# The up blocks' tiles turned by VectorE's 32x32 stream transposes and a trip through DRAM instead of TensorE's turns

## Chip, cores and metric

One core of a Trainium2 chip. The metric is the device time of one execution in microseconds; the median of several executions is given. Lower is better.

## What is computed

Two transformer-like blocks on 256 tokens of width 2048, all in float32, one after the other. What matters here are their two feed-forward parts (`ffn(1, ...)` and `ffn(2, ...)` in the kernel, d_ff = 5632):

```python
h2 = _rmsnorm(x, ffn_norm_w[l])                                     # f = 1
g, u = jnp.split(jnp.einsum('bsd,df->bsf', h2, w_gate_up[l]), 2, axis=-1)
x = x + jnp.einsum('bsf,fd->bsd', jax.nn.silu(g) * u, w_down[l])
...
h2 = _rms(x, g_norm2) * (1 + sc2) + sh2                             # f = 2
gate, up = jnp.split(h2 @ w_ffn_in, 2, axis=-1)
x = x + gt2 * ((jax.nn.silu(gate) * up) @ w_ffn_out)
```

The second block also needs `c_act @ w_ada`, a product with one row (2048 x 12288) that depends on none of the rest.

## The kernel before

**Products.** Each weight matrix is streamed once in units of 1 MB (`raw`, 512 rows by 512 columns, four buffers). A unit has two chunks of 256 rows. For each chunk ScalarE rounds to a high half `whi` (line 903) and VectorE subtracts to get the low half `wlo` (line 1304); four chunk buffers. TensorE forms high x high, high x low and low x high (lines 866 to 868) for two token halves `m` and two k-tiles: 12 products of 128x128 by 128x512 for a chunk. One chunk is one *visit*, and visits set the order of everything: each engine's program is a loop over *slots*, and slot s does its part of visit s. The halves of a chunk are made three visits ahead: in slot s ScalarE casts, and VectorE subtracts, the chunk of visit s+2, whose buffer comes free with the end of visit s-2. On VectorE a slot is: low half, steps of `ada_tiles`, then side work. On ScalarE it is cast, then side work. On TensorE side work comes ahead of the products.

**w_ada.** VectorE forms the one-row product itself, from units of `w_ada` that go through the same four raw buffers (line 1761, two steps in each of two slots per unit). A `w_ada` unit stands after every second weight unit through the whole first feed-forward and the first four of the second one's gate/up pairs (to the middle of the fourth); later there are none.

**Feed-forward.** The 5632 hidden columns are eleven blocks of 512, in parts of six and five. For each j a gate block (8 visits) and an up block (8 visits), then for the part four down blocks of 12 or 10 visits, each over all the hidden columns of the part, in order. Side work of a block is counted by t, from the slot after its last visit: ScalarE's sigmoid and VectorE's multiply for a gate block at t = 0; for an up block, VectorE's multiply at t = 0 (lines 1474, 1476) into `ffn_tmp` (128 tokens by 512 columns, token half m), TensorE's eight turns at t = 2 (line 567 through `turn`, into a PSUM side bank), ScalarE's high half `aH` at t = 2 (line 978), VectorE's low half `aL` at t = 3 (line 1483). `aH` and `aL` (hidden columns on the partitions, tokens along the free axis) are the stationary operands of the down blocks.

**Loads.** SP issues one load per unit in order (line 2094). Load u waits until VectorE has finished with unit u-4 in the same buffer. `after(s)` is the first unit u whose buffer comes free in slot s or later. For an up block whose last visit is e, with `w_ada` units between: unit u-5's buffer comes free in slot e+2, unit u-4 is the `w_ada` unit of slot e+3, u-3 comes free in e+4, and u itself is cast in slots e+7 and e+8. Without them u-4 comes free in slot e+4 and u is cast in slots e+11 and e+12. Here u = `after(e + 3)`.

## Time and profile before

| | |
|---|---|
| median of 3 runs | 2470.77 us (2470.37 to 2470.88) |
| the profiled execution | 2470.06 us, span 2468.2 us |
| TensorE busy | 2460.1 us (100%), granted clock full |
| VectorE, ScalarE, GpSimd busy | 1754.4 (71%), 1191.7 (48%), 26.0 us (1%) |
| chain that ended last | 99% TensorE |
| DMA | 580 MB, 235 GB/s mean, 66% of the engines' time |

The span runs from the first to the last instruction in the trace. Engine rows add up the time in which an instruction of the engine was active. The chain is followed back from the last instruction, at each step to what released it. DVE is VectorE, ACT ScalarE, PE TensorE, PEld its weight loads, SPq the queue from which SP issues DMAs.

### The profile page before, as it was taken

What the parts mean: (1) busy time and instruction counts of PE and PEld (TensorE: products, weight loads), DVE (VectorE), ACT (ScalarE), POOL (GpSimd) and SP (SyncE); (2) the same over time, 40 slices, a digit from 0 to 9 for tenths busy, and PEclk for the clock granted to TensorE, in tenths of its full rate; (3) what the DMA queues carried; (4) which work ended last, traced back from release to release, by engine and by line L of the source; (5) the groups of instructions that cost most, each with busy time, mean ns of one, the idle gap of its engine ahead of it and who ended that gap; (6) DMA issues with size and microseconds to landing.
All of it is one profiled execution on the core that took longest, in us unless ns stands there. A gap on an engine that the chain in (4) does not pass through costs nothing.

```text
span 2468.2 us, 29482 instructions
## 1 busy us (share of the span) xinstructions
PE 2460.1 (100%) x11860; PEld 2158.6 (87%) x11860; DVE 1754.4 (71%) x2173; ACT 1191.7 (48%) x1459; POOL 26.0 (1%) x27
## 2 busy tenths in 40 slices
PE   9999999999999999999999999999999999999999
PEld 8898888888888888888888888888888888888888
DVE  7887798788888788886666465467788765555555
ACT  6545544544444444445765554444644444444443
POOL 0000000000000000000010000000000000000000
PEclk9999999999999999999999999999999999999999
DMA  8656666788888888886455445555588756555564
GB/s 304 236 194 233 224 215 245 257 317 299 289 304 304 307 292 300 303 295 249 164 189 182 155 171 188 205 190 189 190 295 296 286 187 205 201 197 202 193 202 151
DMA packets 82775, 580.27 MB, mean 235 GB/s; under 512 B 9424, under 2 KB 9808, under 8 KB 13264
## 3 DMA queue, kind: packets, MB, share of 16 engines
q1 hardware_dynamic: 82496, 578.28, 66.3%
q8 instruction: 94, 1.54, 0.2%
q14 instruction: 41, 0.34, 0.0%
q10 hardware_dynamic: 144, 0.12, 0.0%
HBM read 576.26 MB, written 2.10 MB: 234 GB/s over the span
## 4 chain that ended last, share of the span: by engine, by line
PE 99%; DVE 0%; DMA 0%; ACT 0%; issue 0%; SPq 0%; POOL 0%; ACTq 0%
PE bank L866 31%; PE bank L867 31%; PE bank L868 31%; PE bank L567 2%; PE bank L647 1%; PE bank L685 0%; DMA raw<-in_w_in_dram 0%; PE bank L696 0%; PE bank L697 0%; PE bank L666 0%; PE bank L655 0%; PE bank L665 0%; PE bank L686 0%; PE bank L708 0%; PE bank L757 0%
## 5 line engine op out<-in xcount | busy, mean ns | idle before, releaser
L1304 DVE TENSOR_TENSOR wlo<-raw,whi 128x1024 fp32r<-128x1024 f32 x885 | 1079.3, 1222 | 622.2 <-ACT whi L903 618.0
L903 ACT CAST whi<-raw 128x1024 fp32r<-128x1024 f32 x885 | 927.2, 1049 | 924.4 <-PE bank L868 907.1
L866 PE MATMUL bank<-whi,hH 128*128 128x512 f32 x2528 | 970.1, 384 | 1.9 <-DVE wlo L1304 1.4
L868 PE MATMUL bank<-whi,hL 128*128 128x512 f32 x2528 | 958.1, 379 | 0.0
L867 PE MATMUL bank<-wlo,hH 128*128 128x512 f32 x2528 | 958.1, 379 | 0.0
L866 PEld LDWEIGHTS bank<-whi,hH 128*128 128x128 f32 x2528 | 477.9, 189 | 69.2 <-DVE wlo L1304 1.8
L868 PEld LDWEIGHTS bank<-whi,hL 128*128 128x128 f32 x2528 | 477.8, 189 | 67.8
L867 PEld LDWEIGHTS bank<-wlo,hH 128*128 128x128 f32 x2528 | 478.1, 189 | 65.1
L1761 DVE SCALAR_TENSOR_TENSOR adacc<-raw,stat,adacc 128x512 f32<-128x512 f32 x360 | 269.5, 749 | 6.8
L866 PE MATMUL bank<-whi,aH 128*128 128x512 f32 x704 | 267.4, 380 | 0.0
L867 PE MATMUL bank<-wlo,aH 128*128 128x512 f32 x704 | 266.8, 379 | 0.0
L868 PE MATMUL bank<-whi,aL 128*128 128x512 f32 x704 | 266.8, 379 | 0.0
L868 PEld LDWEIGHTS bank<-whi,aL 128*128 128x128 f32 x704 | 133.1, 189 | 18.9
L867 PEld LDWEIGHTS bank<-wlo,aH 128*128 128x128 f32 x704 | 133.1, 189 | 18.7
L866 PEld LDWEIGHTS bank<-whi,aH 128*128 128x128 f32 x704 | 133.1, 189 | 18.7
L567 PE MATMUL bank<-ident,tmp 128*128 128x128 f32 x514 | 71.4, 273 | 0.2
L567 PEld LDWEIGHTS bank<-ident,tmp 128*128 128x128 f32 x514 | 61.4, 141 | 10.8 <-issue 0.9
L866 PE MATMUL bank<-whi,mH 128*128 128x512 f32 x128 | 49.2, 384 | 0.0
L867 PE MATMUL bank<-wlo,mH 128*128 128x512 f32 x128 | 48.5, 379 | 0.0
L868 PE MATMUL bank<-whi,mL 128*128 128x512 f32 x128 | 48.5, 379 | 0.0
L978 ACT CAST aH<-bank 128x512 fp32r<-128x512 f32 x44 | 23.8, 592 | 41.5 <-PE bank L567 41.5
L2016 POOL TENSOR_TENSOR stat<-stat 128x4 f32<-128x4 f32 (+2 forms) x22 | 24.0, 1098 | 1729.9 <-DVE stat L1324 1006.7
(311 smaller groups left out, 1416.7 us busy)
## 6 DMA issues: line engine op xcount, KB each, us to landing
raw<-in_w_gu_dram SPq DMA_DIRECT2D x176, 1024.0 KB, 4.9
raw<-in_w_ada_dram SPq DMA_DIRECT2D x96, 1024.0 KB, 4.9
raw<-in_w_down_dram SPq DMA_DIRECT2D x88, 1024.0 KB, 4.8
raw<-in_w_in_dram SPq DMA_DIRECT2D x60, 1024.0 KB, 4.8
raw<-in_w_in2b_dram SPq DMA_DIRECT2D x56, 1024.0 KB, 4.8
raw<-in_w_out_dram SPq DMA_DIRECT2D x32, 1024.0 KB, 4.8
raw<-in_w_in2a_dram SPq DMA_DIRECT2D x8, 1024.0 KB, 4.9
raw<-in_w_mla_dram SPq DMA_DIRECT2D x8, 1024.0 KB, 4.8
```

Of the source, the lines that this page charges most:

```text
L567: return e.transpose(o, i, ident[0:n, 0:n])
L647: ins = e.matmul(o[:, P * hd:P * hd + P], KC[:, base:base + P], qq, start=True, stop=True)
L866: e.matmul(o, xh[:, kt, sl], pairs(wh, i), start=k == 0, stop=False)
L867: e.matmul(o, xh[:, kt, sl], pairs(wl, i), start=False, stop=False)
L868: ins = e.matmul(o, xl[:, kt, sl], pairs(wh, i), start=False, stop=k == n - 1)
L903: e.copy(whi[i][:, :, :], raw[u % RAW][:, 2 * hf:2 * hf + 2, :]).then_inc(*ev("act_hi", c, 0))
L978: e.copy(aH[:, k0:k0 + 4, P * m:P * m + P], v4(side(b.index, m))).then_inc(*ev("act_half", b.index, m))
L1304: e.tensor_tensor(wlo[i][:, :, :], raw[u % RAW][:, 2 * hf:2 * hf + 2, :], f(whi[i][:, :, :]), ALU.subtract).then_inc(*ev("dve_lo", c, 0))
L1761: ins = e.scalar_tensor_tensor(d, src, col, d, ALU.mult, ALU.add)
L2016: e.tensor_tensor(sc(o, n), sc(i, n), sc(b_half, n), ALU.pow).then_inc(*ev("pool_pow", *key))
```

## The change

In an up block VectorE multiplies at t = 0 into a new tile `FT`, in an order in which each group of 32 columns is made of pieces that belong together, then turns every 32x32 block at t = 1 with two stream transposes into `ffn_tmp`. SP stores the two tiles to a DRAM scratch (`across`, 2 x 256 KB), waits for both stores, and loads them back with four transfers, one per 32 partitions, that put the 32x32 blocks where the full transpose has them, into `FT`. The pieces moved are 512 bytes. SP does this ahead of load `after(pl.last + 3)`. ScalarE makes `aH` from `FT` at t = 6 and VectorE `aL` at t = 7. The down blocks wait for `aL` itself. For f = 1 one factor `r2` moves from the up block's multiply into the gate block's, as its square.

```diff
--- before.py
+++ after.py
@@ -373,6 +373,8 @@
         gtB = new("gtB", [P, D])
         gR = new("gR", [P, 2, 16], F32R)
         AUX = [new("aux", [P, 512]), T[4]] + AD
+        FT = new("turned", [P, 2, 512])
+        across = nc.dram_tensor("across", (2, 2, P, 512), F32, kind="Internal").ap()
 
 
         top[0] = arena
@@ -464,6 +466,7 @@
         sem_first = [sem(f"s_first{i}") for i in range(5)]
         sem_xT = [sem(f"s_xT{i}") for i in range(7)]
         sem_x1, sem_vec, sem_late, sem_pos = sem("s_x1"), sem("s_vec"), sem("s_late"), sem("s_pos")
+        sem_away, sem_back = sem("s_away"), sem("s_back")
         sem_ident, sem_fw, sem_am, sem_out = sem("s_ident"), sem("s_fw"), sem("s_am"), sem("s_out")
 
 
@@ -492,6 +495,7 @@
         b_nr = {"q": cols(16), "k": cols(16)}
         b_ni = {k: cols(8) for k in (("q", 0), ("q", 1), ("k", 0), ("k", 1))}
         b_mx = [cols(6) for _ in range(3)]
+        b_rr = cols(2)
 
         def f(ap):
             return ap.bitcast(F32)
@@ -501,6 +505,14 @@
 
         def v8(t):
             return t[:, :].rearrange("p (a b) -> p a b", a=8)
+
+        def by_token(ap):
+
+            return ap.rearrange("p k (i t) -> p i k t", t=32)
+
+        def in_turn(m):
+
+            return FT[:, m, :].rearrange("p (i k t) -> p i k t", i=4, k=4)
 
         def tok_half(t3, m):
             return t3.rearrange("p (a b) -> p a b", a=4)[:, :, P * m:P * m + P]
@@ -548,6 +560,12 @@
 
             return 5 if b.index == 0 else 0
 
+        ups = [b for b in blocks if b.kind == "fup"]
+
+        def landed(b):
+
+            return sem_back, 64 * (ups.index(b) + 1)
+
         def hlev(u):
 
             lev = (u - 3) // 3 - 1
@@ -596,14 +614,6 @@
                 elif kind == "out" and t in (2, 3):
                     e.wait_ge(*on("dve_x1", b.index, 1))
                     turn_pair(lambda m: x[:, m, :], 4 * b.arg[0] + 2 * (t - 2), (b.index, t - 2))
-                elif kind == "fup" and t == 2:
-                    f_, j = b.arg
-                    for m in range(2):
-                        e.wait_ge(*acc_read(b, m))
-                        o = next_bank(e, b.index, m)
-                        for k in range(4):
-                            ins = turn(o[:, P * k:P * k + P], ffn_tmp(j, m)[:, P * k:P * k + P])
-                        ins.then_inc(*ev("pe_turn", b.index, m))
                 elif kind == "latent" and t == 4:
                     for p2 in range(2):
                         e.wait_ge(*on("act_lat", b.index, 1))
@@ -809,8 +819,8 @@
                     e.wait_ge(*side_read(pl.at["out", kt // 4].index, kt % 4 // 2))
                 elif b.kind == "fdown" and b.arg[2] == 0 and i == 0 and kt % 4 == 0 and m == 0:
                     up = pl.at["fup", b.arg[0], PARTS[b.arg[1]][0] + kt // 4].index
-                    e.wait_ge(*side_read(up, 0))
-                    e.wait_ge(*side_read(up, 1))
+                    e.wait_ge(*on("dve_aL", up, 0))
+                    e.wait_ge(*on("dve_aL", up, 1))
                 elif (b.kind == "latent" and b.arg == (0,) or b.kind == "fgate" and b.arg == (2, 0)) and (
                         i == 0 or (kt, m) == (1, 1)):
                     w = 0 if b.kind == "latent" else 1
@@ -970,12 +980,12 @@
                     for m in range(2):
                         e.activation(plain(ffn_tmp(j, m)[:, :]), summed(b, m), ACT.Sigmoid, bias=0.0,
                                      scale=sc(b_r2 + m) if f_ == 1 else 1.0).then_inc(*ev("act_sig", b.index, m))
-                elif kind == "fup" and t == 2:
+                elif kind == "fup" and t == 6:
                     f_, j = b.arg
                     k0 = 4 * (j - PARTS[j >= 6][0])
-                    for m in range(2):
-                        e.wait_ge(*on("pe_turn", b.index, m))
-                        e.copy(aH[:, k0:k0 + 4, P * m:P * m + P], v4(side(b.index, m))).then_inc(
+                    e.wait_ge(*landed(b))
+                    for m in range(2):
+                        e.copy(by_token(aH[:, k0:k0 + 4, P * m:P * m + P]), in_turn(m)).then_inc(
                             *ev("act_half", b.index, m))
                 elif kind == "fdown" and b.arg[:2] == (1, 1) and b.arg[2] < 3 and t == 1:
                     j = b.arg[2]
@@ -1457,31 +1467,42 @@
                     scaled_low(hH, hL, (b.index, t - 3), 4 * b.arg[0] + 2 * (t - 3), "ffn_norm_w")
                 elif kind == "fgate" and t == 0:
                     f_, j = b.arg
+                    if b.arg == (1, 0):
+                        e.wait_ge(*on("pool_pow", "r2"))
+                        e.tensor_tensor(sc(b_rr, 2), sc(b_r2, 2), sc(b_r2, 2), ALU.mult).then_inc(*ev("dve_small", "rr"))
+                        e.wait_ge(*on("dve_small", "rr"))
                     for m in range(2):
                         d, o = plain(ffn_tmp(j, m)[:, :]), summed(b, m)
                         e.wait_ge(*on("act_sig", b.index, m))
                         if f_ == 1:
-                            e.scalar_tensor_tensor(d, o, sc(b_r2 + m), d, ALU.mult, ALU.mult).then_inc(*acc_free(b, m))
+                            e.scalar_tensor_tensor(d, o, sc(b_rr + m), d, ALU.mult, ALU.mult).then_inc(*acc_free(b, m))
                         else:
                             e.tensor_tensor(d, o, d, ALU.mult).then_inc(*acc_free(b, m))
                 elif kind == "fup" and t == 0:
                     f_, j = b.arg
+                    n = ups.index(b)
                     e.wait_ge(*visit(end))
                     for m in range(2):
-                        d, o = plain(ffn_tmp(j, m)[:, :]), summed(b, m)
                         e.wait_ge(*acc_read(pl.at["fgate", f_, j], m))
-                        if f_ == 1:
-                            e.scalar_tensor_tensor(d, o, sc(b_r2 + m), d, ALU.mult, ALU.mult).then_inc(*acc_free(b, m))
-                        else:
-                            e.tensor_tensor(d, o, d, ALU.mult).then_inc(*acc_free(b, m))
-                elif kind == "fup" and t == 3:
+                        if n:
+                            e.wait_ge(*on("dve_aL", ups[n - 1].index, m))
+                        for i in range(2):
+                            s = ffn_tmp(j, m)[:, S * i:S * i + S].rearrange("p (k q c) -> p k q c", k=2, q=4)
+                            d = FT[:, m, :].rearrange("p (q k c) -> p k q c", q=4, k=4)[:, 2 * i:2 * i + 2, :, :]
+                            o = acc(b, m)[:, :].rearrange("p (k q c i) -> p i k q c", k=2, q=4, i=2)[:, i, :, :, :]
+                            ins = e.tensor_tensor(d, o, s, ALU.mult)
+                        ins.then_inc(*acc_free(b, m))
+                elif kind == "fup" and t == 1:
+                    for m in range(2):
+                        e.wait_ge(*acc_read(b, m))
+                        e.transpose(ffn_tmp(b.arg[1], m)[:, :], FT[:, m, :]).then_inc(*ev("dve_turned", b.index, m))
+                elif kind == "fup" and t == 7:
                     f_, j = b.arg
                     k0 = 4 * (j - PARTS[j >= 6][0])
                     for m in range(2):
-                        sl = slice(P * m, P * m + P)
+                        hi, lo = (by_token(w[:, k0:k0 + 4, P * m:P * m + P]) for w in (aH, aL))
                         e.wait_ge(*on("act_half", b.index, m))
-                        e.tensor_tensor(aL[:, k0:k0 + 4, sl], v4(side(b.index, m)), f(aH[:, k0:k0 + 4, sl]),
-                                        ALU.subtract).then_inc(*side_free(b.index, m))
+                        e.tensor_tensor(lo, in_turn(m), f(hi), ALU.subtract).then_inc(*ev("dve_aL", b.index, m))
                 elif kind == "fdown" and b.arg[:2] == (1, 0) and t == 0:
                     j = b.arg[2]
                     e.wait_ge(*visit(end))
@@ -2062,6 +2083,21 @@
                     e.wait_ge(*visit(SK[0] + 16))
                     e.dma_start(amask[:, :, :].rearrange("p a b -> p (a b)"), a["amask"]).then_inc(sem_am, 16)
 
+            def turn_across(u):
+
+                for n, b in enumerate(ups):
+                    if u == after(pl.last[b.index, 1] + 3):
+                        if n >= 2:
+                            e.wait_ge(*landed(ups[n - 2]))
+                        for m in range(2):
+                            e.wait_ge(*on("dve_turned", b.index, m))
+                            e.dma_start(across[n % 2, m], ffn_tmp(b.arg[1], m)[:, :]).then_inc(sem_away, 16)
+                        e.wait_ge(sem_away, 32 * (n + 1))
+                        rows = across[n % 2].rearrange("m (i p) (q c) -> q p m i c", i=4, q=4)
+                        for q in range(4):
+                            e.dma_start(FT[32 * q:32 * q + 32, :, :].rearrange("p m (i c) -> p m i c", i=4),
+                                        rows[q]).then_inc(sem_back, 16)
+
             def after(s):
 
                 return next(u for u in range(RAW, len(pl.units)) if pl.unit_free(u - RAW) >= s)
@@ -2070,6 +2106,7 @@
             for u, (name, k) in enumerate(pl.units):
                 dst = raw[u % RAW][:, :, :].rearrange("p a b -> p (a b)")
                 now_and_then(u, pl.unit_free(u - RAW) if u >= RAW else 0)
+                turn_across(u)
                 if u < 4:
                     if u == 0:
                         for i in range(2):
```

## Rows read from the trace of the kernel before

**Rows 1.** The page: busy times, and the chain that ended last by engine:

```profile
PE 2460.1 (100%) x11860; PEld 2158.6 (87%) x11860; DVE 1754.4 (71%) x2173; ACT 1191.7 (48%) x1459; POOL 26.0 (1%) x27
...
PE 99%; DVE 0%; DMA 0%; ACT 0%; issue 0%; SPq 0%; POOL 0%; ACTq 0%
```

**Rows 2.** Groups by line: busy us, mean ns of one, idle us before, releaser:

```profile
L1304 DVE TENSOR_TENSOR wlo<-raw,whi 128x1024 fp32r<-128x1024 f32 x885 | 1079.3, 1222 | 622.2 <-ACT whi L903 618.0
L866 PE MATMUL bank<-whi,hH 128*128 128x512 f32 x2528 | 970.1, 384 | 1.9 <-DVE wlo L1304 1.4 <-DVE wlo L1292 0.4
...
L903 ACT CAST whi<-raw 128x1024 fp32r<-128x1024 f32 x885 | 927.2, 1049 | 924.4 <-PE bank L868 907.1 <-DMA raw<-in_w_gu_dram 14.8 <-DMA raw<-in_w_in_dram 1.9
...
L567 PE MATMUL bank<-ident,tmp 128*128 128x128 f32 x514 | 71.4, 273 | 0.2
```

**Rows 3.** Two stretches: PE, PEld, DVE, ACT, POOL busy; granted clock, DMA share, GB/s:

```profile
503.00:670.00 167.00, 167.00 (x792) 146.53 (x791) 139.06 (x161) 73.54 (x79) 0.00 (x0) 1.00 0.84 304
2070.00:2200.00 130.00, 130.00 (x608) 113.91 (x607) 71.67 (x67) 54.05 (x54) 0.00 (x0) 1.00 0.59 201
```

**Rows 4.** Landing of all raw loads, 458 to 1110 us:

```profile
DMA to landing us min/median/max: 4.6/5.1/8.6
```

**Rows 5.** ScalarE's timeline round the up block (1, 1):

```profile
602.21 1.05 ACT L903 CAST whi<-raw 128x1024 fp32r<-128x1024 f32 x1 [1.54 <-PE bank L868]
604.80 1.05 ACT L903 CAST whi<-raw 128x1024 fp32r<-128x1024 f32 x1 [1.54 <-PE bank L868]
607.95 1.04 ACT L903 CAST whi<-raw 128x1024 fp32r<-128x1024 f32 x1 [2.10 <-DMA raw<-in_w_gu_dram]
610.42 1.08 ACT L978 CAST aH<-bank 128x512 fp32r<-128x512 f32 x2 [1.42 <-PE bank L567]
```

**Rows 6.** The chain from 609 to 611.5 us: start, us, what:

```profile
609.94 0.87 PE bank L567 x8
610.82 0.22 PE bank L866
```

**Rows 7.** Groups by line and shape on VectorE:

```profile
L1483 DVE TENSOR_TENSOR aL<-bank,aH 128x512 fp32r<-128x512 f32 x44 | 28.2, 682 | 0.0
...
L1769 DVE STREAM_TRANSPOSE tmp<-adacc 128x512 f32<-128x512 f32 x24 | 16.9, 705 | 0.0
...
L1851 DVE TENSOR_TENSOR ybL<-bank,ybH 128x256 fp32r<-128x256 f32 x8 | 3.3, 416 | 0.0
...
L1439 DVE TENSOR_TENSOR mL<-tmp,mH 128x512 fp32r<-128x512 f32 x4 | 2.6, 682 | 0.0
```

**Rows 8.** VectorE's timeline after the up block (1, 1):

```profile
604.80 1.41 DVE L1474 SCALAR_TENSOR_TENSOR tmp<-bank,stat,tmp 128x512 f32<-128x512 f32 x2 [0.29 <-PE bank L868]
606.13 1.22 DVE L1304 TENSOR_TENSOR wlo<-raw,whi 128x1024 fp32r<-128x1024 f32 x1
607.26 1.53 DVE L1761 SCALAR_TENSOR_TENSOR adacc<-raw,stat,adacc 128x512 f32<-128x512 f32 x2
...
613.61 1.28 DVE L1483 TENSOR_TENSOR aL<-bank,aH 128x512 fp32r<-128x512 f32 x2
```

**Rows 9.** Landing of raw loads, 2070 to 2440 us:

```profile
DMA to landing us min/median/max: 4.6/4.8/6.8
```

**Rows 10.** The store out_dram<-x of line 2100 that left at 2463.2:

```profile
L2100 SPq DMA_DIRECT2D out_dram<-x x1: 333/333/333, 2463.2 to 2463.2; - x1
...
DMA to landing us min/median/max: 2.0/2.0/2.0
```

**Rows 11.** DMA from 0 to 30 us; q10 carries the vec load:

```profile
GB/s 0 0 68 229 320 368 333 298 344 369 355 339 289 273 374 401 426 421 407 412 431 421 388 415 421 431 421 437 403 382 428 437 415 393 437 393 437 426 415 415
...
q10 hardware_dynamic: 144, 0.12, 1.6%
```

**Rows 12.** SP's issue of loads u and u+1 at the up block (1, 1):

```profile
611.73 2.32 SPq L2094 DMA_DIRECT2D raw<-in_w_gu_dram  x2
```

**Rows 13.** Landing of the four raw loads issued from 596 to 608 us:

```profile
DMA to landing us min/median/max: 7.0/7.1/8.4
```

## The prediction

> **What bounds the kernel now.** I read the page first. TensorE is busy in 2460 of 2468 us at the full granted clock, and the chain that ended last is TensorE's in 99% of its length [rows 1]: whatever leaves TensorE's stream shortens the kernel, as long as nothing that feeds it becomes late. The feeding chain per chunk is load, ScalarE's high half, VectorE's low half. ScalarE idles 907 us for TensorE (the buffer to come free), VectorE 618 us for ScalarE, so both run ahead of it [rows 2]. Then the table by stage: with the w_ada loads between the weights (up blocks of the first feed-forward) VectorE is busy 139 of 167 us and the DMA engines 84% at 304 GB/s; without them (late in the second) 72 of 130 us and 59% at 201 GB/s [rows 3]. The change puts work on just these two helpers, so the answer depends on the first kind of stretch. There the loads already land in 5.1 us at the median but 8.6 at worst, and one cast waited 2.1 us for a load without TensorE losing anything [rows 4, 5].
>
> **What goes away.** 22 up blocks, 8 turns each, 176 in all. Their price is read from the chain, not from the duration column: the eight take 0.87 us between two products [rows 6], 0.109 us each, though one lasts 273 ns by its own record [rows 2], because they are pipelined. 22 x 0.87 = 19.1 us, all of it on TensorE's path. The Trainium skill ("TensorE: Matmul & The Clock Gate", PE-mode transpose) puts such a turn at about 275 ns in a kernel, most of it access latency; the trace's 273 agrees as a duration, but a sum of 176 such durations would promise 48 us, two and a half times what the chain can give back.
>
> ScalarE's two copies and VectorE's two subtractions stay, with the same sizes, later in the block; their source is SBUF instead of PSUM (128x512 subtract 0.68 us from either [rows 7]).
>
> **What VectorE gets.** The two multiplies become four of 128x256, 0.42 each [rows 7]: 1.68 for 1.41 [rows 8], 0.27 us more. Two stream transposes of 128x512 at 0.70 [rows 7]: 1.41. Together 1.7 us per up block of 41.4 us (16 visits of 2.59, the pitch of the undisturbed casts at 602.21 and 604.80 [rows 5]), VectorE from 83% to 87% in the loaded stretch. The one small product of b_rr is hidden. This busy time costs nothing by itself; what counts is the order.
>
> **One up block, step by step (loaded kind).** I set 0 to the end of its last visit e, 604.80 in [rows 8]. By the plan, SP's place for the new transfers is ahead of load u, which takes the buffer of the w_ada unit that VectorE finishes in slot e+3; load u-1 goes out after the low half of slot e+2; u is first cast in slot e+7, for visit e+9. Fifteen blocks are of this kind (eleven of f=1, the first four of f=2).
> - Multiplies to 1.7, low half to 2.8 (2.55 now), two w_ada steps (1.53) to 4.3, stream transposes done at 5.0 and 5.7.
> - Load u-1 leaves at 2.85 and lands at 7.65, as a lone load does in 4.8 (median of the quiet stretch [rows 9]). The two stores leave at 5.05 and 5.75. A 256 KB store with nothing ahead of it lands in 2.0 us [rows 10]; here it stands behind u-1. From 4.8 for 1 MB and about 420 GB/s, the steady slices of the first 30 us [rows 11], I split a load in 2.5 us of moving and 2.3 fixed, so the 0.5 MB of the stores add 1.25: landed at 8.9. Bounds: 7.75 (behind nothing), 12.4 (u-1 takes the worst 8.6 of [rows 4]).
> - All that time SP waits, and load u waits behind it. Then four issues of 0.33 us each and load u at 10.2; now it leaves at 6.9 (611.73 [rows 12]). This is the real cost: 3.3 us of lateness for one load, and the next (8.9 now) follows at once behind it.
> - Back come 1024 pieces of 512 B. No row shows that size from DRAM in number. Nearest: the vec load, 936 B pieces, 1.6% of 16 engines over 30 us for 144 packets [rows 11], 0.053 us a packet: 64 per engine make 3.4 us. Other bound: full rate, 1.25 us. I take 2.5, nearer to the small packets.
> - Load u lands when both are through: 8.9 + 2.3 + 2.5 + 2.5 = 16.2 (15.0 to 17.1 by that bound alone).
> - Deadline: visit e+9 starts eight visits after 604.60, at 20.55; cast 1.05 [rows 5], low half 1.22 [rows 8] and hand-overs before it leave 18.2. Margin 2.0 us. The cast itself is late by 3.2 us (its nominal start is 13.0), but the three chunks ahead swallow it. ScalarE's wait for the transfer back comes after this cast in the same slot, and the transfer has landed earlier than u, so this wait is never the last. VectorE gets it back by about 1.2 us every two slots.
>
> So nothing is lost in the plain case. When the DMA is in a slow phase (u-1 late by 3.5 us) u lands at 19.7 and TensorE waits 1.5. I allow 2 us for one or two such blocks of fifteen.
>
> **Where the halves are late.** The last up of a part feeds the down block that follows. With five up blocks (second parts) its rows are needed in the ninth visit, at 20.55. Block (1,10), loaded: cast of u 16.2 to 17.25, two copies 1.08 [rows 5] to 18.3; cast of slot e+8 to 19.4; on VectorE low half to 18.5, w_ada to 20.0, low half to 21.2, two subtractions (1.28 [rows 8]) to 22.5. TensorE waits 1.9 us, once. Block (2,10) is without w_ada: transposes done by 4.2, stores landed by about 9, back by 14 to 15, halves by 19 to 20: it just fits. In first parts (six up blocks) two more visits are left.
>
> The seven unloaded blocks keep about 0.87 each: their load u has two more visits, and copies at 14.0 lose at most one more.
>
> **Sum.** -19.1 + 1.9 + 2.0 = -15.2. The profiled execution took 2470.06 us (span 2468.2), 0.7 below the median of the runs; from the median 2470.8 this gives 2455.5.
>
> **Rivals.**
> 1. Loads late in every loaded block, slower. Place: SP's wait for the stores. It decides once u lands over 2.0 us later than worked out; each further us then costs 15. For: the four landings of 7.0 to 8.4 us from 596 to 608 [rows 13], 304 GB/s already, the unmeasured 512 B pieces. Against: bandwidth in total suffices (12 loads at 2.5 and 3.75 for the change in 41.4 us). If u lands 3.6 later (19.8), 15 x 1.6 = 24: 2470.8 - 19.1 + 24 + 1.9 = 2478; if 4.5 later, 2491.
> 2. Half of that: stalls of 0.5 to 1.2 us a block, 8 to 18 in sum, 2461 to 2472. It shades into no change.
> 3. The pieces crawl, slower by far. If the transfer back takes four times what vec's packets say, 14 us, it lands 11.3 later than worked out: load u misses its deadline by 9.3 us in fifteen blocks; in the seven others ScalarE stands at its wait until 25.8, copies, and casts 6.1 us too late. 140 + 43: 2635. Only if 512 B pieces with three strides on the DRAM side are another matter than vec's rows. The Trainium skill ("VectorE: DVE Perf Modes", The three transpose paths) says that a plain copy that transposes by strides is 19 times slower than the transposing transfer when the innermost destination stride is large; an estimate by that rule, 24 us in place of 1.25, gives some 2855. No row here shows such a transfer, and the innermost run is 128 elements on both sides, so this rival gets little.
> 4. The turns' time doesn't come back: TensorE waits anyway for what they gave cover to. Against: before the 2528 products of line 866 TensorE idles 1.9 us in the whole kernel [rows 2], so little of anything stands there to take over the gap. 2471.
>
> **Chances.** Hidden, as worked out: 0.58, with a range of its own of 2450 (no stall at all gives 2451.7) to 2461. Rival 2: 0.14, of it 0.05 still faster and 0.02 slower. Rival 1: 0.22. Rival 3: 0.03. Rival 4: 0.03. A change of 0.2% (5 us) is about what a measurement of this kernel tells from none: faster 0.63, same 0.10, slower 0.27. The range for 8 in 10 reaches from 2450 up to 2482, into rival 1.
>
> **What would show it.** In the profile after: turns fewer by 176 and 22 gaps of 0.87 gone from the chain; stores landed near 9 after the block's end; load u leaving near 10; the casts of slot e+7 waiting some 3 us for a load, with TensorE's products following without idle time; one idle piece near 2 us in the first down block after (1,10). Wrong: TensorE idle for low halves in each block (rival 1), ScalarE's aH waiting for the transfer (rival 3), or stores landing later than 11.

## Result, and the profile after

The changed kernel takes 2497.19 us (median of 4 runs, 2495.49 to 2498.96) against 2470.57 (4 runs, 2470.14 to 2470.88): ratio 1.0108, 95% interval 1.0096 to 1.0121. It is slower by 27 us; the forecast range for 8 in 10 ended at 2482. Forecast were 2455.5 and, as rival 1, 2478 to 2491 with loads late in every loaded block. Rival 1's mechanism is what happened, at a somewhat higher price than its upper number. The profiled execution took 2495.49 us.

The page of the kernel after, its header, chain, groups (busy us, mean ns of one, idle us before and releaser) and DMA issues (count, KB, us to landing):

```profile
span 2493.7 us, 29349 instructions
...
PE 2452.8 (98%) x11684; PEld 2142.6 (86%) x11684; DVE 1775.3 (71%) x2262; ACT 1184.4 (47%) x1459; POOL 26.2 (1%) x27
...
PE 79%; DVE 10%; DMA 8%; ACT 1%; issue 1%; SPq 1%; POOL 0%; ACTq 0%; DVEq 0%
...
L876 PE MATMUL bank<-whi,hH 128*128 128x512 f32 x2528 | 972.6, 385 | 25.4 <-DVE wlo L1314 24.9
...
L876 PE MATMUL bank<-whi,aH 128*128 128x512 f32 x704 | 268.0, 381 | 7.0 <-DVE aL L1505 5.7
...
raw<-in_w_gu_dram SPq DMA_DIRECT2D x176, 1024.0 KB, 5.6
raw<-in_w_ada_dram SPq DMA_DIRECT2D x96, 1024.0 KB, 6.8
...
across<-tmp SPq DMA_DIRECT2D x44, 256.0 KB, 5.7
turned<-across SPq DMA_DIRECT2D x88, 128.0 KB, 2.5
```

The 176 turns are gone (11860 to 11684 instructions), but TensorE now idles 40.9 us (span less busy) where it idled 8.1 [rows 1]. The idle time ends with a low half of VectorE; ahead of the products of the first group it was 1.9 us [rows 2]. DMA holds 8% of the chain. The transfer back is quick, 2.5 us; the w_ada loads land in 6.8.

The same stretches as in [rows 3] (PE, PEld, DVE, ACT, POOL busy; granted clock, DMA share, GB/s):

```profile
503.00:670.00 167.00, 163.17 (x753) 141.16 (x751) 135.15 (x169) 67.42 (x73) 0.00 (x0) 1.00 0.86 314
2070.00:2200.00 130.00, 130.00 (x604) 113.82 (x604) 72.44 (x68) 52.70 (x51) 0.00 (x0) 1.00 0.60 210
```

TensorE loses 3.8 us in the loaded stretch and nothing in the other. The DMA share has hardly risen (0.84 to 0.86). VectorE is not the bound.

The loaded up block of [rows 5, 8, 12] again (counted from (1, 0) it is the third, (1, 2); the text ahead calls it (1, 1)). SP's queue, then ScalarE, then VectorE:

```profile
609.42 0.33 SPq L2131 DMA_DIRECT2D raw<-in_w_ada_dram  x1
611.57 0.85 SPq L2094 DMA_DIRECT2D across<-tmp  x2
617.65 1.80 SPq L2098 DMA_DIRECT2D turned<-across  x4
619.50 0.92 SPq L2131 DMA_DIRECT2D raw<-in_w_gu_dram  x2
620.46 0.43 SPq L2131 DMA_DIRECT2D raw<-in_w_ada_dram  x1
```

```profile
624.59 1.05 ACT L913 CAST whi<-raw 128x1024 fp32r<-128x1024 f32 x1 [7.43 <-DMA raw<-in_w_gu_dram]
625.54 1.13 ACT L988 CAST aH<-turned 128x512 fp32r<-128x512 f32 x2
```

```profile
606.85 1.41 DVE L1493 TENSOR_TENSOR turned<-bank,tmp 128x256 f32<-128x256 f32 x4
...
610.77 1.30 DVE L1498 STREAM_TRANSPOSE tmp<-turned 128x512 f32<-128x512 f32 x2
...
625.67 1.23 DVE L1314 TENSOR_TENSOR wlo<-raw,whi 128x1024 fp32r<-128x1024 f32 x1 [5.12 <-ACT whi L913]
...
630.15 1.29 DVE L1505 TENSOR_TENSOR aL<-turned,aH 128x512 fp32r<-128x512 f32 x2
```

With 0 at VectorE's first multiply (606.85): load u-1 leaves at 2.6, the stores at 4.7 and 5.3, both have landed at 10.8, the four issues back take 1.8, load u leaves at 12.65 and is followed at once by two more loads. The cast of u stands 7.4 us for it. In no loaded block does ScalarE wait for the transfer back (in the whole kernel once, 0.6 us, in (2, 4)). The fourteen other loaded blocks look alike: the stores' landing lets SP go on 9.2 to 12.9 us after the multiply (median 11.2), load u leaves at 13.2 at the median, its cast starts at 16.7 to 21.1. TensorE idles 0.5 to 3.6 us for low halves in thirteen of the fifteen blocks, 24.8 us in sum, 5.7 us once for `aL` after (1, 10), and 2.3 us once, at 1990, for VectorE's last part of w_ada.

What decides when the stores land is load u-1. The next fence has the load u-1 of (1, 2), then load u-1 and the two stores of (1, 7), each with its landing:

```profile
L2131 SPq DMA_DIRECT2D raw<-in_w_ada_dram x1: 328/328/328, 609.4 to 609.4; - x1
DMA to landing us min/median/max: 6.9/6.9/6.9
...
L2131 SPq DMA_DIRECT2D raw<-in_w_ada_dram x1: 328/328/328, 954.4 to 954.4; - x1
DMA to landing us min/median/max: 5.3/5.3/5.3
...
L2094 SPq DMA_DIRECT2D across<-tmp x2: 326/326/327, 956.5 to 957.1; - x2
DMA to landing us min/median/max: 3.6/3.8/4.0
```

In (1, 2) load u-1 lands at 616.3 and SP goes on at 617.65, 1.3 us later. In (1, 7) it lands at 959.7 and the stores at 961.0 or 961.1, again 1.3 later. In thirteen of the fifteen blocks this distance is 1.3 or 1.4 us; it is 2.6 in (1, 6) and 4.7 in (1, 0), where a load of `final_norm_w` stands between load u-1 and the stores and lands 1.3 us ahead. Load u-1 takes 5.1 to 8.0 us, median 7.2. In (1, 7), with its 5.3, SP goes on at 9.2 and TensorE does not idle.

The end of the part, block (1, 10): part of the chain from 1095 us (start, us, what), and then the windows round it (columns as above):

```profile
1095.34 5.23 DMA raw<-in_w_down_dram
...
1106.05 0.70 DVE aL L1505
1106.75 0.14 issue
1106.88 0.77 PE bank L876
1107.65 0.43 PE bank L877
...
1110.18 0.21 PE bank L877
```

```profile
1100.00:1110.00 10.00, 4.32 (x13) 3.23 (x12) 8.21 (x10) 4.92 (x6) 0.00 (x0) 0.83 0.95 367
1110.00:1120.00 10.00, 10.00 (x48) 8.76 (x47) 7.19 (x10) 6.23 (x12) 0.00 (x0) 1.00 0.74 262
```

After 5.7 us without a product TensorE's next ones follow each other at 0.43 us for some 3 us, then at 0.22 again: the lower of its two levels (1.2 GHz), and the granted clock of that stretch is 0.83. So an idle piece can cost more than its own length. There are four such stretches, behind idle pieces of 3.1 us (block (1, 4)), 2.4 (1, 6), 5.7 (1, 10) and 2.3 (at 1990):

```profile
712.00:722.00 10.00, 6.95 (x25) 5.47 (x24) 7.18 (x9) 6.07 (x8) 0.00 (x0) 0.83 0.89 351
925.00:935.00 10.00, 7.63 (x28) 6.10 (x27) 7.10 (x9) 6.07 (x8) 0.00 (x0) 0.83 0.87 343
1102.00:1112.00 10.00, 5.12 (x17) 4.27 (x18) 8.39 (x10) 4.27 (x6) 0.00 (x0) 0.83 0.95 365
1987.00:1997.00 10.00, 7.73 (x29) 6.17 (x28) 9.15 (x14) 3.70 (x5) 0.00 (x0) 0.83 0.78 283
```

A granted clock of 0.83 over 10 us is 1.7 us of work lost, 6.8 in the four. From 625 to 640 us, round the 0.5 us of (1, 2), the granted clock stayed at 1.00, and so it did from 1850 to 1860 and from 1940 to 1950, round pieces of 2.8 and 2.5 us.

### The profile page after: what moved, and what is told of

Read it like the earlier page. It is cut to its first block, busy times and chain, and to the rows that moved or that the text cites. A ratio compares the mean times of both kernels' runs of the same rounds, so it can differ in the third digit from the quotient of the medians.

```text
span 2493.7 us, 29349 instructions
## 1 busy us (share of the span) xinstructions
PE 2452.8 (98%) x11684; PEld 2142.6 (86%) x11684; DVE 1775.3 (71%) x2262; ACT 1184.4 (47%) x1459; POOL 26.2 (1%) x27
## 4 chain that ended last, share of the span: by engine, by line
PE 79%; DVE 10%; DMA 8%; ACT 1%; issue 1%; SPq 1%; POOL 0%; ACTq 0%; DVEq 0%
PE bank L876 25%; PE bank L877 25%; PE bank L878 25%; DMA raw<-in_w_gu_dram 5%; DVE wlo L1314 4%; DVE adacc L1782 3%; DMA across<-tmp 2%; PE bank L585 2%; PE bank L657 1%; ACT whi L913 1%; DMA raw<-in_w_down_dram 1%; SPq L2098 1%; DVE turned L1493 1%; DVE aL L1505 1%; DVE tmp L1498 1%
## 5 line engine op out<-in xcount | busy, mean ns | idle before, releaser
L878 PE MATMUL bank<-whi,hL 128*128 128x512 f32 x2528 | 959.7, 380 | 0.0
L877 PEld LDWEIGHTS bank<-wlo,aH 128*128 128x128 f32 x704 | 133.5, 190 | 18.8
L585 PE MATMUL bank<-ident,tmp 128*128 128x128 f32 x338 | 48.6, 273 | 0.2
L585 PEld LDWEIGHTS bank<-ident,tmp 128*128 128x128 f32 x338 | 40.8, 141 | 8.6 <-issue 0.9
L1493 DVE TENSOR_TENSOR turned<-bank,tmp 128x256 f32<-128x256 f32 x88 | 31.1, 417 | 3.1 <-PE bank L878 3.1
```

The costliest lines, as they stand in the source:

```text
L585: return e.transpose(o, i, ident[0:n, 0:n])
L877: e.matmul(o, xh[:, kt, sl], pairs(wl, i), start=False, stop=False)
L878: ins = e.matmul(o, xl[:, kt, sl], pairs(wh, i), start=False, stop=k == n - 1)
L1493: ins = e.tensor_tensor(d, o, s, ALU.mult)
```

## Experiments

Each ratio is to the kernel before, timed on the same chip in the same rounds (2470.1 to 2470.4 us). Theory: SP stands still until the stores have landed, in a stretch where a load can bear only little lateness. Rivals: the small pieces, the bytes, VectorE's extra work, or the late halves.

**No transfer.** No store, no wait and no transfer back; the halves are made from the tile that is not turned. The upper bound of the gain.

```diff
-                    e.wait_ge(*landed(b))
+                        e.wait_ge(*on("dve_turned", b.index, m))
-                turn_across(u)
```

> The changed kernel without its stores to DRAM and its transfer back; the high and low halves are made from the multiplied tile, so the output is another (the 32x32 blocks stay where they are and the down blocks get values that are not transposed). VectorE's four multiplies and two stream transposes stay, TensorE's turns stay out. Every theory: if the turns cost TensorE 0.87 us a block, all of it comes back: 2470.6 - 19.1 = 2451.5 (2450 to 2454). If VectorE's extra 1.7 us a block were what makes the changed kernel slow, it would stay near 2490.

2451.08 us, ratio 0.9923 (0.9908 to 0.9937): 19.3 us less than before (2470.36 in the same rounds). Its page:

```profile
PE 2441.7 (100%) x11684; PEld 2141.1 (87%) x11684; DVE 1781.4 (73%) x2262; ACT 1193.4 (49%) x1459; POOL 26.0 (1%) x27
```

So the turns are worth what the chain's price said, 22 x 0.87 = 19.1, and the extra work of VectorE costs nothing. Everything lost, 44.3 us between the two spans (2449.4 and 2493.7), comes with the transfers. It is 33.2 us of idle TensorE and 11.1 us more busy time for the same 11684 instructions. Of the latter 6.8 are the four stretches at the lower clock. Some 3 more are an estimate from the records: a product's record lasts 0.38 us while the next one starts after 0.22, so that each of some twenty idle pieces costs 0.16 more than the gap between the records. The last 1.3 are open. The multiplies of the same blocks in the two traces lie 22.1 us apart at (1, 10), 28.3 at (2, 0) and 44.3 at (2, 4), and stay 44.3 apart to the end: about 3 us per loaded block, none in the seven others.

**Stores and wait alone, on the kernel before.** TensorE's turns stay; the two stores go out where the change has them, and SP waits for them. Nothing comes back.

```diff
+                        for m in range(2):
+                            e.wait_ge(*on("pe_turn", b.index, m))
+                            e.dma_start(across[n % 2, m], ffn_tmp(b.arg[1], m)[:, :]).then_inc(sem_away, 16)
+                        e.wait_ge(sem_away, 32 * (n + 1))
```

> The kernel before, all its turns kept, with two stores of the same tiles to DRAM at the place on SP where the changed kernel has them, and SP's wait for their landing; nothing is loaded back. The stores leave 6.1 us after the block's end (when the turns are done; 4.7 to 5.3 in the changed kernel). Theory S: load u leaves near 12, about 1 us earlier than in the changed kernel, so TensorE waits less in each of fifteen blocks: 2474 to 2490. Theory B, the pieces of 512 B being the trouble: 2470 to 2474; B with any traffic being the trouble: 2480 to 2490.

2471.05 us, ratio 1.0002 (0.9993 to 1.0012). SP's queue at (1, 2), the multiply there at 605.84:

```profile
608.40 0.33 SPq L2110 DMA_DIRECT2D raw<-in_w_ada_dram  x1
611.49 0.80 SPq L2077 DMA_DIRECT2D across<-tmp  x2
614.61 0.81 SPq L2110 DMA_DIRECT2D raw<-in_w_gu_dram  x2
```

The stores leave 3.1 us after load u-1 instead of 2.1, and load u leaves at 8.8. That lateness of 1.9 us against before is inside the margin. This block is one of the quick ones: in the fifteen loaded blocks load u leaves 8.7 to 14.8 us after the multiply, median 9.5, against 13.2 in the change. Load u-1 takes 5.7 us at the median here, 7.2 there. So SP's wait is shorter in this run than in the change, and it doesn't price that one.

**All the traffic, on the kernel before**: the same, and the four transfers back behind the wait, which nobody reads.

```diff
+                        e.wait_ge(sem_away, 32 * (n + 1))
+                        rows = across[n % 2].rearrange("m (i p) (q c) -> q p m i c", i=4, q=4)
+                        for q in range(4):
+                            e.dma_start(FT[32 * q:32 * q + 32, :, :].rearrange("p m (i c) -> p m i c", i=4),
+                                        rows[q]).then_inc(sem_back, 16)
```

> The kernel before, all turns kept, with all of the changed kernel's DMA work at its place on SP: two stores (leaving at 5.7 after the block's end), SP's wait for them, the four transfers back in 512 B pieces, into a tile that nobody reads; none of VectorE's new work. e1 and after stand 46.1 us apart. If that is the DMA part alone (wait, issues, traffic), this kernel shows most of it, though its blocks are 0.87 us longer and give that much more room (13 us over fifteen blocks): 2495 to 2517. If it takes VectorE's later low halves as well to do the harm: 2471 to 2480.

2488.43 us, ratio 1.0072 (1.0055 to 1.0089): 18 us slower with nobody waiting for the result. Late halves are not needed to explain a loss. In the trace (its profiled execution took 2497.69 us) load u-1 takes 7.2 us at the median again and load u leaves at 13.1, as in the change.

**The traffic without the wait**: the four transfers read weights in place of the scratch, so they need not wait for the stores, and SP looks for those only two loads later. Load u leaves at 9.0 at the median.

```diff
+                        src = a["w_gu"][n:n + 2, :, 0:512]
+                        rows = src.rearrange("m (i p) (q c) -> q p m i c", i=4, q=4)
...
+                    if u == after(pl.last[b.index, 1] + 3) + 2:
+                        e.wait_ge(sem_away, 32 * (n + 1))
```

> As b3_all_dma, but the four transfers take their 512 B pieces from a weight matrix in DRAM instead of what was stored, so SP needs no wait between stores and transfers: the same bytes, pieces and issues, without the wait (and another place of the data in DRAM). Load u leaves near 8.4. Theory S (the wait): 2470 to 2474. Theory B (the traffic): close to b3_all_dma.

2470.84 us, ratio 1.0004 (0.9995 to 1.0014). The same bytes in pieces of the same size cost nothing that can be told from none; ScalarE's casts wait 109 us for loads from 458 to 1130 us, and the chunks ahead swallow nearly all of that. Stores with their wait 0.7 us, traffic without it 0.6 (neither clear of zero), both 18: the price is not a sum but that of a margin exceeded. One thing besides the wait differs: these transfers read another place in DRAM, not what was just written. No run tells what that is worth.

**2 KB pieces back** (rows stay where they were, so the blocks are not moved).

```diff
-                        rows = across[n % 2].rearrange("m (i p) (q c) -> q p m i c", i=4, q=4)
+                        rows = across[n % 2].rearrange("m (q p) c -> q p m c", q=4)
```

> The changed kernel with the same four transfers back and the same bytes, but in pieces of 2 KB, each to where it came from, so the blocks stay untransposed and the output is another. 256 packets for 1024. Theory S: the transfer back lands at most 1 us earlier, the wait stays: 2485 to 2497. If the small pieces hold up load u by their number (theory B): 2455 to 2475.

2490.84 us, ratio 1.0083 (1.0068 to 1.0098): 6 of the 46 us between no transfer and the change. The transfer back lands in 2.6 us, as before in 2.5. The small pieces are not the main cause.

**Load u ahead of the wait.** Stores where they were; the wait and the transfer back go behind load u.

```diff
-                    if u == after(pl.last[b.index, 1] + 3):
+                    u0 = after(pl.last[b.index, 1] + 3)
+                    if u == u0:
...
+                    if u == u0 + 1:
```

> The changed kernel, with SP's wait for the stores and the transfer back put behind load u instead of ahead of it (stores, load u, wait, back, load u+1). The same bytes in the same pieces. Theory S (the cost is load u, held back on SP until the stores have landed and the four issues are made, some 6 us): u+1 is needed 5.2 us later than u, so nearly all goes away: 2452 to 2462. Theory B (the cost is the traffic itself: 1 MB more per block, half of it in 512 B pieces, on DMA engines already 84% busy): 2485 to 2500 as now.

2465.67 us (2460.24 to 2475.19, 10 runs), ratio 0.9987 (0.9974 to 1.0000). One load moved past the wait gives 31.5 of the 46.1 us back: most of the loss hangs on the wait in front of load u. 14.6 us over no transfer stay. The transfer back now lands in 3.9 us at the median (3.1 from 458 to 1130 us, where `aH` waits 10.2 us for it).

**Two loads ahead of the wait** (`u0 + 2` in place of `u0 + 1`).

> As e2_back_after_one, with the wait and the transfer back put behind load u+1 too. e2 keeps 14.6 us over e1. If that rest is load u+1 held back (13 instead of 8.9) and the casts behind it, it shrinks: 2453 to 2460. If it is the late halves aH and aL (transfer back landing later still): 2466 to 2480.

2509.24 us, ratio 1.0172 (1.0152 to 1.0193), far above both expectations. The waits from 458 to 1130 us (engine line waited for: us in total, times, longest):

```profile
ACT aH L988 <- DMA turned<-across: 59.8, 11, 6.3
...
PE bank L876 <- DVE aL L1505: 7.7, 1, 7.7
```

The waits for loads are 125.5 us in that stretch, 204.0 in the change: one load further and ScalarE stands for the transfer back, with all its casts behind it.

**A queue of its own.** The stores, the wait and the transfer back are issued by GpSimd; SP issues loads alone.

```diff
+            def turn_across(n, b):
...
+            for n, b in enumerate(ups[:11]):
+                turn_across(n, b)
...
-                turn_across(u)
```

> The changed kernel with stores, wait and transfer back issued by GpSimd, which is idle there; SP issues only the loads. Same bytes, same pieces. Theory S: 2452 to 2462, if GpSimd's way of issuing is not slower than some 4 us. Theory B: 2485 to 2500.

2531.36 us, ratio 1.0239 (1.0221 to 1.0257). The two transfers on its page:

```profile
across<-tmp POOLq DMA_DIRECT2D x44, 256.0 KB, 4.6
turned<-across POOLq DMA_DIRECT2D x88, 128.0 KB, 6.7
```

**ScalarE's queue**: stores at t = 2, wait and transfer back at t = 5, issued by ScalarE.

```diff
+                elif kind == "fup" and t == 5:
+                    n = ups.index(b)
+                    e.wait_ge(sem_away, 32 * (n + 1))
...
-                turn_across(u)
```

> The changed kernel with the same stores and transfers issued by ScalarE from its own queue: the two stores in its slot t = 2 of the up block, the wait for them and the four transfers back at t = 5; SP issues only loads, in order, with no wait between. Theory S: load u leaves at 6.9 to 8.7 again; ScalarE's cast of slot e+4 is about 1.2 us late and its wait at t = 5 (from 11.5) finds the stores landed; 2451.1 of e1 plus at most 6 for late halves at the ends of the second parts: 2452 to 2458. If it is the traffic beside the loads: as e2, 2461 to 2475. If ScalarE's issues and waits hold up the casts: over 2470.

2555.05 us, ratio 1.0347 (1.0332 to 1.0361). ScalarE's timeline at (1, 1):

```profile
580.29 2.42 ACTq L993 DMA_DIRECT2D turned<-across  x4
584.06 1.04 ACT L913 CAST whi<-raw 128x1024 fp32r<-128x1024 f32 x1 [4.26 <-DMA raw<-in_w_gu_dram]
593.52 1.14 ACT L1000 CAST aH<-turned 128x512 fp32r<-128x512 f32 x2 [8.41 <-DMA turned<-across]
```

Both free SP of the wait and both are the slowest of all. The transfer back, 2.5 us on the queue that the wait had emptied, takes 6.7 and 6.9 beside SP's loads. The Trainium skill ("DMA: Bandwidth & Descriptors", Issuing engines are not separate DMA queues) says that transfers started by different engines end up on the same 16 DMA engines and interleave; the trace agrees in so far as the two queues slow each other, at 6.7 and 6.9 us against 2.5. From 458 to 1130 us `aH` waits 76.7 us for the transfer back in the one run and 82.1 in the other: the small transfer, which is the urgent one, is what suffers.

**Early stores.** The stream transposes move to t = 0, the stores ahead of load u-1, wait and transfer back ahead of load u, `aH` to t = 5 and `aL` to t = 6.

```diff
-                elif kind == "fup" and t == 1:
...
+                    u0 = after(pl.last[b.index, 1] + 3)
+                    if u == u0 - 1:
...
+                    if u == u0:
```

> The changed kernel with the same work in another order: VectorE's stream transposes right behind the multiplies (t = 0, ahead of the low half), the stores ahead of load u-1 instead of behind it, wait and transfer back ahead of load u as before, aH at t = 5 and aL at t = 6. Worked out as in the prediction with what the runs showed: transposes done at 2.1 and 2.7 after the block's end, stores out at 2.8 with no load just issued ahead of them, landed near 6; load u-1 out at 4.0 (2.6 now); back out at 6.0 to 7.8; load u, whose buffer is now free at 8.2, at 8.3 in place of 13.0, so it lands some 4 us ahead of its deadline; the transfer back stands only behind u-1 and lands near 11, ahead of ScalarE's wait at 11.5. Theory S: nothing lost in any block: 2451 to 2456. If traffic beside the loads costs by itself: 2460 to 2475.

2476.41 us, ratio 1.0022 (1.0011 to 1.0033). From 458 to 1130 us SP's wait for stores falls from 61.2 to 39.2 us and ScalarE's for loads from 204.0 to 128.7; load u leaves at 9.9 at the median, not at the 8.3 expected. But the transfer back now stands behind load u-1: it takes 3.7 us at the median there (4.9 in the whole kernel), and `aH` waits 45.2 us for it.

**Early stores, 2 KB pieces** (both edits).

> The early order of the experiment before this one (stream transposes at t = 0, stores ahead of load u-1, wait and transfer back ahead of load u, aH at t = 5, aL at t = 6), with the transfer back in whole rows of 2 KB in place of pieces of 512 bytes. The 32x32 blocks are then left where they were, so that aH and aL hold other elements than the reference's; the work and the bytes are the same. It tells apart why the transfer back took 4.9 us at the median there and 2.5 us in the changed kernel. Theory A, small pieces lose against the 2 KB packets of load u-1 on the same 16 engines: then with 2 KB pieces the transfer back lands in under 3.5 us also beside a load, ScalarE's aH waits 10 us or less for it instead of 45 (458 to 1130 us), and the time is 2455 to 2462. Theory B, whatever stands behind a load in flight is late, and the piece size is not the matter: the transfer back still lands in 4.5 to 5 us, aH waits some 40 us, and the time is 2470 to 2476.

2475.65 us, ratio 1.0020 (1.0010 to 1.0029). The two pages have, of the early stores and of this one:

```profile
turned<-across SPq DMA_DIRECT2D x88, 128.0 KB, 4.9
```

```profile
turned<-across SPq DMA_DIRECT2D x88, 128.0 KB, 4.6
```

`aH` waits 42.5 us instead of 45.2, and from 458 to 1130 us the transfer back takes 4.0 us at the median instead of 3.7. So its pieces being small is not what makes it slow. That leaves the load in flight ahead of it (theory B).

**One hop.** SBUF to SBUF without DRAM or a wait for stores: sixteen transfers of 32 partitions, eight ahead of load u, eight ahead of u+1.

```diff
+                            for i in range(4):
+                                if (4 * q + i) * 2 // 16 != u - u0:
+                                    continue
+                                e.dma_start(FT[32 * q:32 * q + 32, :, 128 * i:128 * i + 128],
+                                            TW[b.arg[1] % 2][32 * i:32 * i + 32, :, 128 * q:128 * q + 128]).then_inc(
+                                    sem_back, 16)
```

> The changed kernel with one hop instead of two: sixteen transfers per up block straight from SBUF to SBUF, one per 32x128 strip of both token halves, 512 B pieces, eight ahead of load u and eight ahead of load u+1; no store, no wait on SP but that for the stream transposes, nothing through DRAM. Theory S: no wait for a store; but 8 issues of 0.33 us put load u at 5.3 + 2.9 = 8.2 and u+1 at 11.5, both inside their margins: 2452 to 2462. Theory B (traffic of small pieces): half the bytes through the queue, 2470 to 2485.

2473.05 us, ratio 1.0014 (1.0004 to 1.0023). The wait is gone, but eight issues take SP 5.1 us (0.64 each), so load u still leaves at 10.4 to 11.1 and u+1 at 16.1 to 16.8.

**Only in the seven unloaded up blocks**; the fifteen others keep TensorE's turns.

```diff
-        ups = [b for b in blocks if b.kind == "fup"]
+        ups = [b for b in blocks if b.kind == "fup"][15:]
```

> The changed kernel with the new way only in the seven up blocks that have no w_ada loads beside them (f = 2, from the fifth on), TensorE's turns kept in the fifteen others. The trace of the changed kernel puts all of its loss in those fifteen: 2470.3 - 7 x 0.87 = 2464.2 (2463 to 2466). If the loss were spread over all blocks: 2470 to 2478.

2464.23 us (2463.58 to 2464.48, 8 runs), ratio 0.9975 (0.9965 to 0.9985). It beats both kernels, the one before by 6.0 us (2470.22 in the same rounds); 7 x 0.87 = 6.1. From 2000 to 2440 us no cast of its trace waits for a load. (The order with load u ahead of the wait has a median near it, but its runs spread over 15 us.)

## Why the prediction was wrong

**The turns, right.** 19.1 worked out, 19.3 measured with no transfer, 6.0 for seven blocks (6.1 worked out). VectorE's 1.7 us per block is free, as said.

**The step that failed: "Load u-1 leaves at 2.85 and lands at 7.65, as a lone load does in 4.8".** It leaves at 2.6 and lands in 7.2 us at the median, so at 9.8. It isn't a lone load: in (1, 2) the loads u-3 and u-2 left at 604.7 and 605.8 and are in flight with it. The 4.8 came from the quiet stretch [rows 9], where loads don't overlap so. In the kernel before, the loads u-1 of the eleven blocks of the first feed-forward took 4.7 to 7.4 us, median 5.7, and [rows 13] showed four landings of 7.0 to 8.4 just here. The prediction had them in hand as "worst" and as evidence for rival 1, and still summed with the quiet value. The second half of the step, 1.25 us more for the stores' bytes, was right to a tenth (1.3). The stores landed at 11.2 at the median, past the 11 that the prediction had named as a sign of being wrong.

The rows of this place would not have been enough either: 5.7 us makes load u 0.9 late, inside the margin of 2.0. The rest of the 7.2 comes with the change, for without transfers the same fifteen loads took 4.7 to 5.8 us, median 5.2. Two things about it show in the traces. Load u-2 leaves later: 1.0 to 1.6 us ahead of the multiply in eight of those eleven blocks, where before it left 2.8 ahead in nine, so more of it is still in flight. And the stores behind a load slow it: in the six blocks from (2, 5) on, with no other load in flight, load u-1 takes 5.7 to 6.0 us with the stores 0.65 us behind it, 4.7 to 5.3 before. How the 7.2 divides between them isn't shown. The prediction let the change's traffic meet the old timing, and left out that lateness and traffic may feed each other, as these traces suggest.

**From the stores' landing to load u's**: 7.3 worked out (2.3 + 2.5 + 2.5), 7.6 measured at the median, but as another sum, so partly by luck: 1.8 for the four issues (1.3 worked out; 0.45 each, against 0.33 for a load) and then 5.6 for load u itself. Load u leaves at 13.2 in place of 10.2 and lands at 18.8 in place of 16.2. Of these 2.6 us 2.3 are the stores' landing.

**What each late microsecond costs.** "Each further us then costs 15" held for the idle time. The casts of u start at 18.8 at the median where 16.2 was worked out, 2.6 later. To that comes the lateness of VectorE itself: in (1, 2) its multiply follows the low half at once with no wait for TensorE, where in [rows 8] it had waited 0.29, and it starts 1.1 to 1.4 us after its block's end in six of the eleven blocks of the first feed-forward and 2.4 in (1, 4), 0.9 on the mean. That makes 3.5 us, 1.5 over the margin, and 15 x 1.5 = 22; measured were 24.8. Block by block it fits better still. Take the start of u's cast after the block's end and subtract the prediction's deadline of 18.2: this gives 0.7 us for (1, 2), 3.2 for (1, 4), 1.5 for (1, 5), 2.5 for (1, 6) and nothing for (1, 7). TensorE idled 0.5, 3.1, 1.3, 2.4 and nothing. In all thirteen blocks with idle time for low halves the first piece agrees to 0.2 us.

**What rival 1 left out.** Lateness outlives its block: (1, 10) cost 5.7 instead of 1.9, the w_ada part came 2.3 late, and with the idle pieces came 11.1 us more busy time, 6.8 of it the lower clock, of which the prediction has no term. 2451.1 without transfers, + 24.8 + 5.7 + 2.3 + 11.1 gives 2495.0; the profiled execution took 2495.5.

**Rival 3, the crawling pieces, didn't occur.** Each of the four transfers back lands 2.5 us after its issue, fixed time included, and 2.6 with 2 KB pieces; 2.5 without the fixed time was taken. The rule of the Trainium skill ("VectorE: DVE Perf Modes", The three transpose paths) on strided copies holds for a large innermost destination stride; here the innermost run is 128 elements side by side, so this transfer neither bears it out nor refutes it. (By the prediction's own terms 14 us are 11.5 over the 2.5, not 11.3, and its upper bound for the stores is 12.7, not 12.4; nothing hangs on either.) **Rival 4** is refuted by the run without transfers.

**Where the change's gain could have been kept.** The seven unloaded blocks keep their 6.0 us. For the fifteen others no order that was tried keeps anything: the best, load u ahead of the wait in all 22 blocks, is 4.7 us under the kernel before (2470.36 in its rounds), less than the seven blocks give alone. The loads should not stand behind a wait for stores, and the transfer back should not stand behind loads; each of the other five orders that moved or took away SP's wait shows more waiting of `aH` (45.2 to 82.1 us from 458 to 1130 in four of them) or more issue time of SP (one hop). That one or the other must happen in every order is argued, not shown. Not settled is why the transfer back is still slower on a second queue (6.7, 6.9) than behind one load on the same (3.9 to 4.9); 2 KB pieces were not tried there.

## What to carry over

Price a wait on the load queue by what is in flight at that very place, not by a lone transfer: here the queue went on 1.3 us after the load ahead of the stores had landed, and that load took 7.2 us, not 4.8. Expect the change to slow it too. A store, wait, load-back trip is free where the queue has spare visits, and dear in stretches where a load can bear only two microseconds; so make such a change by stage, and compare by stage. And read the landing of the neighbouring transfers, block by block: a median over the stretch hid that in five of eleven blocks load u-1 already took 6.6 us or more.

## What the runs showed of the hardware

- A 256 KB store that leaves 0.65 us after a 1 MB load lands in 5.6 to 5.8 us (the change, blocks (2, 5) to (2, 10); here and in what follows the first store of the two), one that leaves 3.2 us after it in 2.1 to 2.5 (stores and wait alone, the same blocks), and one with nothing in flight in 2.0 (early stores, same blocks; the second store there 2.2). The transfer back of 4 x 128 KB: 2.5 us on an emptied queue, 4.8 to 5.3 when it leaves 1 us behind a load (early stores, the first three of each four in the same blocks). Pieces of 2 KB instead of 512 B moved its page medians by 0.1 and 0.3 us.
- A transfer that leaves behind a load doesn't always land behind it: in the one-hop kernel the 32 KB transfers that left 2.7 us after load u-1 of (1, 2) landed in 2.5 us, 1.8 ahead of that load.
- Beside 1 MB loads on SP's queue, the same 128 KB transfers took 6.7 us from GpSimd's queue and 6.9 from ScalarE's.
- An issue took SP 0.33 us for a whole tile, 0.45 for a strided quarter, and 0.64 for a 32-partition strip between two places in SBUF.
- After TensorE's idle piece of 5.7 us its products came every 0.43 us instead of 0.22 for some 3 us. The same followed pieces of 3.1, 2.4 and 2.3 us, but not those of 2.8 and 2.5.
